# Inverse roots from Ln and Exp with one ScalarE table set, in a two-block transformer kernel

## The reference

```
rms_norm(x, g) = x * rsqrt(mean(x*x) + 1e-6) * g
block 1: h = rms_norm(x) modulated;  x += swiglu(h)               (norm 0, feed-forward 0)
         h = rms_norm(x) modulated;  x += hybrid_mixer(h) @ w_o   (norm 1, attention)
           8 stick-breaking heads: log sigmoid of scores, reverse cumulative sum, exp
           8 forgetting heads: q and k each rms-normed per head, softmax with a decay
         h = rms_norm(x) modulated;  x += swiglu(h)               (norm 2, feed-forward 1)
block 2: 16 meta tokens are put ahead of x;  u = rms_norm(h)      (norm 3); z = u @ w_in
         y_gla = linear attention in chunks of 64; o * rsqrt(mean(o*o)) * gain * silu(r)
         y_mla = softmax attention on latents, rms_norm(q_lat), rms_norm(kv_lat)
         h += [y_gla, y_mla] @ w_out
         h += top-2-of-64 experts of width 512 (routing by top_k on rms_norm(h)); rms_norm(h)
```

## Time and profile before

| | us |
|---|---|
| median of three runs | 2514.72 |
| span of the profiled execution, first to last instruction | 2512.3 |
| TensorE busy | 2202.1 (88%) |
| VectorE busy | 1046.5 (42%) |
| ScalarE busy | 538.1 (21%) |
| DMA share in the last 15 of 40 slices | over 90% |

### The profile page before, as it was taken

One profiled execution on the slowest core, in us unless ns is written; L12 is line 12 of the kernel. 1 busy time (PEld: TensorE's weight loads), 2 busy tenths in 40 slices (PEclk: granted clock), 3 DMA queues, 4 the chain that ended last, 5 costly groups with the idle time before them and its releaser, 6 DMA issues.

```text
span 2512.3 us, 34448 instructions
## 1 busy us (share of the span) xinstructions
PE 2202.1 (88%) x14459; PEld 1539.3 (61%) x14459; DVE 1046.5 (42%) x1740; ACT 538.1 (21%) x1049; POOL 0.2 (0%) x4
## 2 busy tenths in 40 slices
PE   8999999998889899999999998777777777777776
PEld 5888888665564788888754554544444444444443
DVE  4767643245563634453234734323333222222223
ACT  3111100355241211110121321111121111111112
POOL 0000000000000000000000000000000000000000
PEclk8999999999899999999999998989998888898998
DMA  7565621412102134212401032899999999999997
GB/s 272 187 216 186 225 93 46 101 51 62 56 1 67 34 101 133 82 47 92 144 14 67 1 155 101 340 428 428 429 428 428 429 428 428 429 428 428 429 428 300
DMA packets 149365, 549.05 MB, mean 219 GB/s; under 512 B 8320, under 2 KB 101776, under 8 KB 123552
## 3 DMA queue, kind: packets, MB, share of 16 engines
q1 hardware_dynamic: 149280, 547.82, 55.2%
HBM read 545.70 MB, written 2.10 MB: 218 GB/s over the span
## 4 chain that ended last, share of the span: by engine, by line
PE 61%; DMA 29%; DVE 5%; ACT 3%; issue 1%; SPq 1%; PEldq 0%; ACTq 0%; DVEq 0%; PEld 0%
DMA slots<-in_expert_w_up 27%; PE ps L821 20%; PE ps L864 11%; PE ps L1355 7%; PE ps L911 3%; PE ps L1276 2%; PE ps L1002 2%; PE ps L1081 2%; PE ps L1076 1%; PE ps L917 1%; PE ps L935 1%; DMA slots<-in_w_mod 1%; PE ps L1079 1%; PE ps L1221 1%; DVE big L2025 1%
## 5 line engine op out<-in xcount | busy, mean ns | idle before, releaser
L1355 PE MATMUL ps<-slots,xT 128*32 128x256 f32 x4052 | 296.0, 455 | 196.0 <-DMA slots<-in_expert_w_up 175.8
L1355 PEld LDWEIGHTS ps<-slots,xT 128*32 128x32 f32 x4052 | 154.4, 130 | 324.9 <-DMA slots<-in_expert_w_up 183.3
L821 PE MATMUL ps<-hT,slots 128*128 128x256 f32 x1408 | 316.2, 383 | 4.6 <-ACT hT L1471 4.5
L821 PEld LDWEIGHTS ps<-hT,slots 128*128 128x128 f32 x1408 | 270.3, 192 | 43.8 <-issue 4.9
L821 PE MATMUL ps<-slots 128*128 128x256 f32 x1056 | 237.8, 382 | 4.2 <-DVE slots L1869 4.2
L821 PEld LDWEIGHTS ps<-slots 128*128 128x128 f32 x1056 | 200.9, 191 | 31.9 <-issue 4.7
L2390 DVE COPY hT<-ps 128x128 f32<-128x128 f32 x64 | 18.5, 289 | 419.9 <-PE ps L1362 419.9
L2396 DVE TENSOR_TENSOR big<-ps,big 128x512 f32<-128x512 f32 x128 | 88.3, 691 | 222.7 <-PE ps L1388 222.7
L1738 ACT ACTIVATE xT<-ps 32x256 f32<-32x256 f32 x256 | 96.0, 375 | 262.1 <-PE ps L1373 259.8
L1373 PE MATMUL ps<-slots,hT 128*32 128x256 f32 x2048 | 123.8, 381 | 31.1 <-DVE hT L2390 29.0
L1732 ACT ACTIVATE big<-ps 32x256 f32<-32x256 f32 x128 | 47.9, 374 | 400.5 <-PE ps L1355 399.7
(11 more groups left out here) (377 smaller groups left out, 2730.6 us busy)
## 6 DMA issues: line engine op xcount, KB each, us to landing
slots<-in_expert_w_down SPq DMA_DIRECT2D x64, 2048.0 KB, 24.9
slots<-in_expert_w_gate SPq DMA_DIRECT2D x63, 2048.0 KB, 18.6
slots<-in_expert_w_up SPq DMA_DIRECT2D x63, 2048.0 KB, 23.0
slots<-in_w_mod SPq DMA_DIRECT2D x18, 2048.0 KB, 11.8
slots<-in_w_gate SPq DMA_DIRECT2D x22, 1024.0 KB, 5.3
slots<-in_w_up SPq DMA_DIRECT2D x22, 1024.0 KB, 8.0
slots<-in_w_down SPq DMA_DIRECT2D x8, 2816.0 KB, 10.1
slots<-in_w_in SPq DMA_DIRECT2D x24, 512.0 KB, 5.7
```

Source lines behind the costliest of these rows:

```text
L821: last = mm(bank[:, g], lhs[:, g, k], rhs[:, k], start=(first and g == 0 and k == 0), stop=(k == 3), skip_group_check=True)
L1355: last = mm(ps[at:at + CAP, j, 0:256], xsT[:, k, i * CAP:(i + 1) * CAP], w[g][k][:, 256 * h:256 * (h + 1)], start=(k == 0), stop=(k == KC ...
```

## The change

Every Sqrt but the two of single columns late in block 2 (L1711, L1765) becomes Ln with the same scale and bias, followed on ScalarE by Exp with scale -0.5; VectorE's reciprocals behind them go (L1834, L2065, L2169, L2170, L2210). The gate's 1/(1+exp(-r)) becomes Exp, Ln with bias 1, Exp with scale -1 on ScalarE; L2186 and L2187 go. The dummy root on L1445 goes. The table set that holds Ln and Exp is loaded by hand at the start of the program, and at the head of norms 1 and 3. TensorE's waits that protected PSUM bank 7 look at the Ln now (s_qln), not at the finished root.

```diff
+            nc.scalar.preload_act_table_set(LN_EXP)      # first instruction of ScalarE
...
                 if r == 0:
                     act.wait_ge(s_o, 1)
-                av(fox_s[:, 15:16], eps_col[:, 0:1], ACT.Sqrt)
+                elif r != 2:
+                    nc.scalar.preload_act_table_set(LN_EXP)
...
                     act.wait_ge(s_ss, KC - 1 + std_count(r, b))
-                    av(rstd[:, h0:h0 + w], ps[:, b, 0:w], ACT.Sqrt, scale=1.0 / D, bias=eps_col[:, 0:1]).then_inc(s_std, 1)
+                    av(rstd[:, h0:h0 + w], ps[:, b, 0:w], ACT.Ln, scale=1.0 / D, bias=eps_col[:, 0:1]).then_inc(s_lv, 1)
+                    act.wait_ge(s_lv, std_count(r, b))
+                    av(rstd[:, h0:h0 + w], rstd[:, h0:h0 + w], ACT.Exp, scale=-0.5).then_inc(s_std, 1)
...
             def deviation(p, m):
-                av(eb[:, m, :], ps[:, 7, :], ACT.Sqrt, scale=1.0 / HD, bias=eps_col[:, 0:1]).then_inc(s_qstd, 1)
+                av(eb[:, m, :], ps[:, 7, :], ACT.Ln, scale=1.0 / HD, bias=eps_col[:, 0:1]).then_inc(s_qln, 1)
+                act.wait_ge(s_qln, 2 * (p - 4) + m + 1)
+                av(eb[:, m, :], eb[:, m, :], ACT.Exp, scale=-0.5).then_inc(s_qstd, 1)
...
-                av(gexp, gr[:, 2 * pair:2 * pair + 2, :], ACT.Exp, scale=-1.0).then_inc(s_gex, 1)
+                link(av(gexp, gr[:, 2 * pair:2 * pair + 2, :], ACT.Exp, scale=-1.0))
+                link(av(gexp, gexp, ACT.Ln, bias=1.0))
+                av(gexp, gexp, ACT.Exp, scale=-1.0).then_inc(s_gex, 1)
...
-            av(tmp[:, 1, 0:SEQ], ps[:, 4, :], ACT.Sqrt, scale=1.0 / 256, bias=eps_col[:, 0:1])
-            av(halves(tmp[:, 0, :]), ps[:, 6:8, 0:264], ACT.Sqrt, scale=1.0 / P, bias=eps_col[:, 0:1]).then_inc(s_lstd, 1)
+            # the same two with Ln, then two Exp of scale -0.5, the last with .then_inc(s_lstd, 1)
...
-                av(orst, ps[:, 2, :], ACT.Sqrt, scale=1.0 / P, bias=eps_col[:, 0:1]).then_inc(s_gstd, 1)
+                link(av(orst, ps[:, 2, :], ACT.Ln, scale=1.0 / P, bias=eps_col[:, 0:1]))
+                av(orst, orst, ACT.Exp, scale=-0.5).then_inc(s_gstd, 1)
...
                     dve.wait_ge(s_std, std_count(r, b))
-                    link(v.reciprocal(rstd[:, t0:t0 + w], rstd[:, t0:t0 + w]))
...
-            def inverse(p, m):
-                dve.wait_ge(s_qstd, 2 * (p - 4) + m + 1)
-                link(v.reciprocal(eb[:, m, :], eb[:, m, :]))
-
             def normed(p, m):
                 dve.wait_ge((s_qc, s_kc)[m], p + 1)
+                dve.wait_ge(s_qstd, 2 * (p - 4) + m + 1)
...
-                if h % 2 == 0 and 4 <= p + 1 < N_PAIR:
-                    inverse(p + 1, 0)
                 if n >= 8:
...
                     normed(p + 1, 0)
-                    inverse(p + 1, 1)
                     normed(p + 1, 1)
...
-            v.reciprocal(tmp[:, 1, 0:SEQ], tmp[:, 1, 0:SEQ])
-            link(v.reciprocal(tmp[:, 0, :], tmp[:, 0, :]))
...
-                link(v.tensor_scalar(gexp, gexp, 1.0, None, ALU.add))
-                link(v.reciprocal(gexp, gexp))
...
             def gla_head(h):
                 dve.wait_ge(s_gstd, h + 1)
-                link(v.reciprocal(orst, orst))
```

More of the change, by code:

```diff
@@ L22 @@
 EPS = 1e-6
+LN_EXP = "natural_log_exp_and_others"
 HD = 64
@@ L216, in build @@
         s_ss = sem("square_sum_done")
-        s_std = sem("std_ready")
+        s_std = sem("inverse_std_ready")
+        s_lv = sem("log_mean_square_ready")
         s_nx = sem("normed_ready")
@@ L240, in build @@
         s_qn = sem("qk_normed")
-        s_qstd = sem("qk_std_ready")
+        s_qstd = sem("qk_inverse_std_ready")
+        s_qln = sem("qk_log_mean_square_ready")
         s_z = sem("scores_done")
@@ L977, in first_half @@
                     else:
-                        pe.wait_ge(s_qstd, 2 * (n - 4))
+                        pe.wait_ge(s_qln, 2 * (n - 4))
                     project(n, 0, 7).then_inc(s_q, 1)
@@ L990, in second_half @@
                     pe.wait_ge(s_qsq, 2 * (n - 4) + 2)
-                    pe.wait_ge(s_qstd, 2 * (n - 4) + 1)
+                    pe.wait_ge(s_qln, 2 * (n - 4) + 1)
                     mm(ps[:, 7, :], const("head_ones"), eb[:, 1, :], start=True, stop=True).then_inc(s_qss, 1)
@@ L1044, in _ @@
                         else:
-                            pe.wait_ge(s_qstd, 8)
+                            pe.wait_ge(s_qln, 8)
                         mix(d, bank, 0, 4).then_inc(s_wo, 1)
@@ L1643, in _ @@
             act.wait_ge(s_lss, 1)
-            av(tmp[:, 1, 0:SEQ], ps[:, 4, :], ACT.Sqrt, scale=1.0 / 256, bias=eps_col[:, 0:1])
-            av(halves(tmp[:, 0, :]), ps[:, 6:8, 0:264], ACT.Sqrt, scale=1.0 / P, bias=eps_col[:, 0:1]).then_inc(s_lstd, 1)
+            av(tmp[:, 1, 0:SEQ], ps[:, 4, :], ACT.Ln, scale=1.0 / 256, bias=eps_col[:, 0:1])
+            link(av(halves(tmp[:, 0, :]), ps[:, 6:8, 0:264], ACT.Ln, scale=1.0 / P, bias=eps_col[:, 0:1]))
+            av(tmp[:, 1, 0:SEQ], tmp[:, 1, 0:SEQ], ACT.Exp, scale=-0.5)
+            av(tmp[:, 0, :], tmp[:, 0, :], ACT.Exp, scale=-0.5).then_inc(s_lstd, 1)
             unit_copy(U_GQ)
```

## The result

The changed kernel takes 2472.54 us (median of 4 runs, 2471.75 to 2481.14) beside 2515.24 us (4 runs, 2514.41 to 2516.82) for the kernel before, on one chip: ratio 0.9836, 95% interval 0.9825 to 0.9848. The forecast was 2478.5 us in a range of 2472 to 2490. The profiled execution took 2473.32 us for a span of 2471.3 us, and before 2514.7 for 2512.3, so the span is 41.0 us shorter where the forecast's sum was 36.2.

What follows compares the result with a forecast made beforehand. TensorE's products, and for 27% the experts' incoming weights, were taken as the bound. 26.0 us of TensorE's waits plus 10.2 of clock, 36.2 us, cut the span from 2512.3 to 2476.1; with 2.4 for the median, 2478.5, range 2472 to 2490.

Steps and rivals of the forecast that it cites:

- Stick-breaking heads: Five attention heads: with the load before Ln gone, TensorE's waits before a turn go, 3.5 us in all.
- Head 7 to head 8: Before scores(8): two loads (2.57 us) and VectorE's two 3.34 us reciprocals leave the chain, 9.3 us sooner.
- Forgetting heads: Heads 8, 10, 12: without q's reciprocal ahead of masked_max, values come 2.3 us sooner, three times: 6.9 us.
- The clock: TensorE's granted clock returns to full after head 7's long wait (5.1 us) and around three values (1.7 each): 10.2 us.
- The rival without it: Rival: the waits go but TensorE's granted clock does not come back; 26.0 us gained, 2488.7 us, chance 0.22.
- Norms: Norms 1 to 3: Exp replaces the reciprocal before scaling; 1.3, 1.3 and 1.0 us, sum 3.6 us; norm 0 nothing.
- Linear-attention heads: Waits of 1.2 us in head 1 and 1.5 us at head 3's end go: 2.7 us.
- Gate and latents: Their work lies under projections in which TensorE waits for neither: worth nothing; 13 us due were that cover gone.
- The end: Experts' stage: first expert load issued near 1445 us instead of 1481.27, the same 1031 us from there to the end.
- Absorbed: Rival: something other than the latent attention's end starts the experts' loads, hiding all gain: 2514.7 us, chance 0.03.
- the further quad of experts: Rival: changed bits move router choices, an expert gets a 33rd row, one more 64 us quad: 2542 us, chance 0.03.
- loads put back: Rival: the build puts a load between Ln and Exp of each inverse root: 2504 us, chance 0.06.

Runs made afterwards that it cites:

- e6: The kernel before with the common Ln/Exp table set loaded in attention, all roots and reciprocals kept: 2504.92 us, ratio 0.9966.
- e1: The changed kernel without its three table loads, the build placing every load: 2505.78 us, ratio 0.9957 to the kernel before.
- e2: The kernel before with q's reciprocal moved behind masked_max and head_copy in heads 8, 10 and 12, nothing removed: 2516.09 us, ratio 1.0.
- e4: The changed kernel with the gate pair's sigmoid as before, VectorE's reciprocals back: 2477.97 us, ratio 0.985 to the kernel before.
- e5: The changed kernel run once more, nothing edited: 2473.8 us, ratio 0.9841 to the kernel before.
- e7: The kernel before with the attention part of the change alone; norms, latents, gate and linear-attention heads as before: 2484.96 us, ratio 0.9881.
- e8: The changed kernel with root and reciprocal back in norms 0 to 3, common set reloaded behind norms 1 and 3: 2483.74 us, ratio 0.9879.
- e11: The changed kernel run again, nothing edited: 2473.15 us, ratio 0.9838 to the kernel before.
- e3: The changed kernel with head_copy ahead of masked_max on VectorE in heads 8, 10, 12 and 14: 2469.33 us, ratio 0.981 to the kernel before.

## Why the prediction was right

The reading that carried it held: the sum is made at TensorE's waits and not of busy time. The two engines have 114 us less work together, and the span is 41 us shorter. The steps, by its own terms:

- **Stick-breaking heads.** Right: 3.7 against 3.5 us, the wait and not the load. e6, which takes the loads away and nothing else, has the same 3.7. The loads there were 1.28 us each in five chains, and TensorE's own work covered the rest.
- **Head 7 to head 8.** Right, 9.3 us, and the two causes separate as told: the loads are 2.6 of it (e6: 2.9 sooner in head 7's turn, the 7.1 us wait before scores(8) still there), the reciprocals the rest. e1, where the loads are back and only the reciprocals are gone, shows that rest alone: 6.8 us by scores(8), where the forecast had 2 x 3.35.
- **Forgetting heads.** 7.2 against 6.9, with 1.2 us of wait left for 1.3. The text gave the gain to the q reciprocal ahead of masked_max alone and called the second one worth nothing "there". e2 shows what that hides: with both reciprocals kept, in the new order, the next scores come 2.3 us late and nothing is gained. The price was right; its reason, the order of one reciprocal, was half of it.
- **The clock.** Taken in full at 10.2, measured 9.5 in attention (4.6 + 4.9). The rival without it, 2488.7, is out. That it came back whole at head 8 is in part luck of the execution: the reason given, that the waits left would be nearer to the short ones, holds for the values (clock 1.00 around them in the first trace, and in e4, e5, e7, e8 and e11 too), but behind the same 1.7 and 0.3 us only 1.3 of the 4.6 us came back in e3, e4, e5 and e8. The forecast had 0 or all, and the runs show a third outcome.
- **Norms.** The mechanism was right, the first product 1.1 to 1.2 us sooner each time. The size was off where the clock is touched: norm 1 kept only 0.7 in the first pair of traces (0.9 in e8's), norm 3 gave 2.9 with its clock. The forecast had put those 1.7 us into the range's lower end and not into the sum.
- **Linear-attention heads.** 3.1 against 2.7, and 1.8 us of clock that had likewise been kept for the range. Both waits of the earlier trace rows are gone.
- **Gate and latents.** Nothing, as forecast; e4 shows it for the gate, within its stretch. The latents were not tried alone.
- **The cost side.** 39.0 us less on ScalarE against 36 forecast, 9 loads left as listed.
- **The end.** SyncE's first expert load is issued at 1441.82 instead of 1481.27 us, forecast "near 1445", and from there to the end are 1029.5 us (forecast 1031):

```profile
1441.82 0.43 SPq L687 DMA_DIRECT2D slots<-in_expert_w_gate  x1
```

"Absorbed" is thereby out, and so is the further quad of experts, which would have made that stretch 64 us longer.

What the forecast missed is the half clock at the end of the latent attention, 4.2 us. It isn't to the change's credit either, as e5 shows, and the late start (+2.5 us) hid part of it. With both set aside the pair of traces gives 39.3 us, of which 3.5 are the clock behind norm 3 and the linear-attention heads. The measured 2472.54 us lies 6 us under the forecast and only half a microsecond inside its range, and these clock terms are most of the difference.

The rival "loads put back" priced at 2504 what e1 measured at 2505.78. Its terms stand in the main: against the trace of before, e1 has nothing in the stick-breaking heads (forecast 0), gains 6.8 us by scores(8) (6.7), and then 4.6 of clock and 6.2 at the values with theirs (6.9, and 5 of clock for both), and loses 9.4 in three norms (7.5).

On the switch between table sets: in e1 the Exp's 0.42 us from 463.87 end at 464.29, the load starts at 464.31, and the next Ln starts at 465.60 behind its 1.28 us. A switch is 1.3 us from one activation's end to the next one's start. The Trainium skill (ScalarE: Activation LUTs, "What ACT_TABLE_LOAD costs") has the 1283 ns of the load and a drain of some 1380 ns besides. The trace agrees with the first and has no room for the second: of e1's 67 loads, 53 stand with less than 0.1 us to the activation on either side, and each of those switches took 1.31 to 1.39 us.

## What to carry to other kernels

Before a reciprocal or a table load is priced, find who waits behind it: here 41 loads and 23 reciprocals fewer left two engines with 114 us less work, and were worth 41 us of time, and the same 1.28 us load cost nothing under a scan, a full wait in a norm, and a second wait for the copy queued behind it. A change of functions and the loading of their common set by hand belong together: without the second, the first kept 10 of 42 us. When two edits of one change stand for one wait, like an order and a cheaper instruction, try each alone; e2's order was worth nothing that could be measured (ratio 1.0, 0.999 to 1.0009).

## What the runs showed of the hardware

The granted clock can differ between two executions of one program at the same instruction, with the same waits in front of it: 1.00 and 0.59 over 618 to 625 us, 1.00 and 0.53 over 1438 to 1449 us. Between 1.0 (2.4 GHz) and 0.5 (1.2 GHz) those two places were worth 3.3 and 4.2 us of one execution. A difference of 5 us between two single profiles of this kernel therefore says little, while the shift of the same instruction is steady to about 0.1 us within a stretch where both traces have the same clock (e7 in attention, e4 through the gate's stretch).

Waits of 1.7 us in front of head 8 (L947) with 0.3 us behind it stood beside a full clock in the first trace and beside 0.59 in e5, while the three waits of 1.2 us before the values brought no drift between these two traces. So there are stretches here for which TensorE's waits in the trace don't decide the clock.
